# A transformer layer on one core: single-token attention moved beside a head's projection, attention rows merged per head on GpSimd, head turns written out, input sums of the FFN on TensorE

## The chip, the cores and the metric

The kernel runs as one program on one core of a Trainium2 chip. The core has five engines, each with its own instruction stream: TensorE (PE in the profile; its weight loads are PEld), VectorE (DVE), ScalarE (ACT), GpSimd (POOL) and SyncE (SP, which here only issues DMAs). They order themselves by semaphores. The metric is device time in microseconds, lower is better; the kernel before takes 2558.33 us (median of 3 runs, 2557.53 to 2559.42). `L123` is line 123 of the kernel.

## The reference

One decoder layer (D = 1024) is computed for a prompt of 1024 tokens and for 8 samples of one new token each ("sample attention" below), side by side as 1032 columns.

```
h = rms_norm(x); proj = h @ w_in                       # q/k/v of 3 dilated groups, DeltaNet q/k/v/z, gates
o_a = dilated attention, 3 groups, 4 heads of 64: each group gives o, max and denominator;
      merged per head by softmax over the groups' log-sum-exp
      (samples: 8 queries against 129, 129 and 65 keys per group, from caches; one softmax over all groups)
o_b = gated DeltaNet, 8 heads of 128: causal conv(4) + silu, chunked delta rule, gated rms norm
mix = sigmoid(gate_a) * (o_a @ w_branch_a) + sigmoid(gate_b) * (o_b @ w_branch_b)
x = x + rms_norm(mix @ w_out); h = rms_norm(x)
gt, up = split(h @ w_ffn_in); x = x + rms_norm((silu(gt) * up) @ w_ffn_out)
```

Matrix products are done in three passes of split operands (hi and lo parts, `passes`, L271 to L273). Small products and transposes are plain float32, of which one instruction gives two records in the trace.

## The kernel before, in words

The program is a sequence of blocks; a block ends when all engines have reached its end.

1. `norm_block`, then `attention_block`: prompt attention in three groups. Each query tile's unnormalised rows, denominators and maxima go to DRAM (`att_scr`), rows of 4 heads x 66 numbers.
2. `sample_attention_block` (L899 on): a block of its own. TensorE spreads the 8 queries over the partitions by products with selector rows (L1017), VectorE multiplies them with the cached keys (L946) and sums (L950), the softmax follows on 32 rows, and TensorE does 48 products of 2 columns for the outputs (L1048; 96 records). Beside it VectorE merges the prompt's groups (`merge_steps`, L841 to L866), TensorE transposes the merged rows (L828), and they stay in SBUF as `oaT`.
3. `clear_semaphores` (L100): GpSimd clears 75 semaphores one after the other.
4. `heads_block`: the DeltaNet heads. TensorE first transposes the convolution constants (L1746). Head 0's projection follows alone: four tiles (q, k, v, z) of 24 steps, a step being three 344-column products. Then eight turns: turn i computes head i's recurrence, and between its products TensorE does the six tiles (two gates, q, k, v, z) of head i+1's projection as filler. `Filler` and `per_slot` fix by hand how many steps stand between two products of the recurrence; the other engines' streams are laid out by the same step numbers. Turns 0 to 6 are one hardware loop (`Fori`), turn 7 is written out. GpSimd's stream in a turn: load `s_state`, scale it (L2523), later store it.
5. A second clear (100 semaphores), then `pair_block` "mix": its prelude splits `oaT` into hi and lo (ScalarE, then VectorE).
6. `row_block` "wo", then `ffn_block` (a Winograd-like form with 7 products instead of 8). Before its first product it needs sums and differences of blocks of the normed input: `sums_of_x` (L1244 to L1252) and their split (L1263, L1269), one half on VectorE, the other on GpSimd. The splits of the first weight tile follow (L1370 to L1388). Then `row_block` "fo".

What sets the order everywhere is each engine's written stream and the semaphores; there is no scheduler.

Of the kernel before, what the change touches and what calls it, by code (L numbers as in the profile page):

```python
# [21 lines left out]
NS = 8  # L22
# [56 lines left out]
def build(nc, a, o):  # L79

    ctx = ExitStack()
    with ctx:
# [15 lines left out]
        def clear_semaphores():  # L98
# [8 lines left out]
            live.clear()  # L107

# [152 lines left out]
        oaT = sb(oa_stack, "oaT", [P, 2, T])  # L261
# [151 lines left out]
        qT_s = sb(att_stack, "qT_s", [P, NG, 2, NS])  # L413
# [60 lines left out]
        def attention_block():  # L474

            with ExitStack() as s, nc.Block() as block:
# [18 lines left out]
                os_ = sb(s, "a_os", [P, 2, HA, HS]); nm = sb(s, "a_nm", [P, 2, HA])  # L497
# [6 lines left out]
                KVO = (2, 5, 9)  # L504
                done = sums(NT * [KT + 1])
                SPLIT_Q = 4

# [28 lines left out]
                def _(sp):  # L536
# [14 lines left out]
                    for g in range(NG):  # L551
# [5 lines left out]
                        for t in range(NT + 1):  # L557
                            if t == NT:
                                wt(sp, "kv_ev", g, t + 1)
                                dst = o[("kv128_s", "kv512_s", "kv2048_s")[g]][0, :, 0].rearrange("b s h d -> b (s h d)")  # L560
                                sp.dma_start(dst, kv_s[:, g]).then_inc(kvo[g], 16)
                            elif g == 2:
# [10 lines left out]
                        for t in range(NT):  # L573
                            wt(sp, "oe", g, t + 1)
                            wt(sp, "ex", g, t + 1)
                            sp.dma_start(dram_rows(g, t, att_scr[g]),
                                         os_[:, t % 2].rearrange("p h w -> p (h w)")).then_inc(oso[t % 2], 16)
# [97 lines left out]
                def _(act):  # L675
# [12 lines left out]
                    def exps(g, t):  # L688
                        wt(act, "nm", g, t + 1)
                        nk = len(blocks(g, t))  # L690
                        for h in range(HA):
                            x = sc[t % 2][:, h, (2 - nk) * P:]
                            last = nc.scalar.activation(x, x, ACT.Exp, bias=nm[:, t % 2, h:h + 1],
                                                        accum_out=os_[:, t % 2, h, HD:HD + 1])
# [50 lines left out]
                def _(v):  # L745
                    def out_copy(g, t):
                        wt(v, "pv", g, t + 1)
                        for e in range(2):
                            src = banks[4][:].rearrange("p (m e w) -> p m e w", m=2, e=2)[:, :, e, 64 * e:64 * e + 64]
                            last = nc.vector.tensor_copy(os_[:, t % 2, e::2, :HD], src)  # L750
# [23 lines left out]
                    def tile(g, t, fill):  # L774
# [13 lines left out]
                        inc(nc.vector.reduce_max(os_[:, t % 2, :, HD + 1], sc[t % 2][:, :, ks], AX.X), "mx")  # L788
                        wt(v, "mx", g, t + 1)
                        wt(v, "ex", g, max(t - 1, 0))  # L790
                        inc(nc.vector.tensor_scalar(nm[:, t % 2], os_[:, t % 2, :, HD + 1], -1.0, None, ALU.mult), "nm")
# [15 lines left out]

        def merge_steps(s):

            x = sb(s, "m_x", [P, NG, NT, HA, HS]); top = sb(s, "m_top", [P, NT, HA])  # L810
            f = sb(s, "m_f", [P, NG, NT, HA]); z = sb(s, "m_z", [P, NG, NT, HA])
            y = sb(s, "m_y", [P, NT, HA, HD]); y2 = sb(s, "m_y2", [P, NT, HA, HD])
            ld, dv, ac, tr = sem("m_ld"), sem("m_dv"), sem("m_ac"), sem("m_tr")

            def load(sp):
                for g in range(NG):
                    sp.dma_start(x[:, g].rearrange("p t h w -> p t (h w)"),
                                 att_scr[g].rearrange("(t p) w -> p t w", p=P)).then_inc(ld, 16)

            def exps(act):  # L820
                act.wait_ge(dv, 3)
# [1826 lines left out]
```

## Time and profile before

| | us |
|---|---|
| median of 3 runs | 2558.33 |
| the profiled execution | 2558.09 |
| its span (first to last instruction) | 2556.3 |
| TensorE busy | 2265.0 (89%) |
| VectorE busy | 1285.0 (50%) |
| ScalarE busy | 718.7 (28%) |
| GpSimd busy | 66.4 (3%) |
| mean granted clock of TensorE, as a share of full speed | 0.93 |

Engines overlap, so busy times do not add up to the span. "Idle before, releaser" in a row is the time for which the engine waited just before that group and who ended the wait. The granted clock of TensorE has two levels here, 1.0 (2.4 GHz) and 0.5 (1.2 GHz).

### The profile page before, as it was taken

Reading aid. Unit: us, or ns where it says so; the run is one execution under the profiler, and the core shown is the slowest. Engines: PE = TensorE matmul, PEld = TensorE weight load, DVE = VectorE, ACT = ScalarE, POOL = GpSimd, SP = SyncE. Lnnn points to the kernel's source line nnn. Section 1 sums busy time; section 2 is a strip of 40 time slices with the busy share of each in tenths; the row PEclk is TensorE's granted clock in tenths of the full one; section 3 lists DMA queues with packets and bytes.
Section 4 is the critical chain, followed back from the end, with each engine's and each line's share of the span. In section 5 each row is a group of like instructions: output and inputs, shape, how many; then the busy total and the mean of one; then the engine's idle time right before and its main releaser. Section 6 shows DMA issues by size and latency. Waiting matters only on the chain. (4 is left out here: it accounts for less than half of the span.)

```text
span 2556.3 us, 37393 instructions
## 1 busy us (share of the span) xinstructions
PE 2265.0 (89%) x14464; PEld 2099.3 (82%) x14464; DVE 1285.0 (50%) x2344; ACT 718.7 (28%) x1590; POOL 66.4 (3%) x40
## 2 busy tenths in 40 slices
PE   5888988568999999999999779692999999979898
PEld 3677877458999999999999679571999999958676
DVE  4123221244766667666676623358666666531233
ACT  4122221102342323423224210353332233231221
POOL 0000000000000000000000000005000000000000
PEclk9989998558999999999999989896999999989999
DMA  4010201313121212212122144430222222150432
GB/s 147 22 64 11 81 11 51 100 48 77 46 61 43 79 45 59 61 43 79 46 58 69 58 143 138 161 119 25 67 85 81 80 74 74 58 175 23 141 111 63
DMA packets 209582, 190.39 MB, mean 74 GB/s; under 512 B 30243, under 2 KB 180804, under 8 KB 209478
## 3 DMA queue, kind: packets, MB, share of 16 engines
q1 hardware_dynamic: 196090, 144.12, 19.3%
q10 hardware_dynamic: 11120, 36.96, 3.7%
q0 software_dynamic: 2304, 8.39, 1.4%
q8 instruction: 44, 0.72, 0.1%
q14 instruction: 24, 0.20, 0.0%
HBM read 138.05 MB, written 51.59 MB: 74 GB/s over the span
## 5 line engine op out<-in xcount | busy, mean ns | idle before, releaser
L271 PE MATMUL bank<-xT_hi,w_lo 128*128 128x344 f32 x1152 | 393.7, 342 | 3.6 <-DVE w_lo L267 3.6
L273 PE MATMUL bank<-xT_hi,w_hi 128*128 128x344 f32 x1152 | 368.6, 320 | 0.0
L272 PE MATMUL bank<-xT_lo,w_hi 128*128 128x344 f32 x1152 | 368.5, 320 | 0.0
L271 PEld LDWEIGHTS bank<-xT_hi,w_lo 128*128 128x128 f32 x1152 | 218.0, 189 | 3.7 <-issue 3.7
L272 PEld LDWEIGHTS bank<-xT_lo,w_hi 128*128 128x128 f32 x1152 | 218.1, 189 | 0.0
L273 PEld LDWEIGHTS bank<-xT_hi,w_hi 128*128 128x128 f32 x1152 | 217.0, 188 | 0.0
L1293 PE MATMUL bank<-xT_hi,f_hi 128*128 128x258 f32 x704 | 199.5, 283 | 0.0
L1289 PE MATMUL bank<-xT_hi,f_lo 128*128 128x258 f32 x704 | 199.3, 283 | 0.0
L1291 PE MATMUL bank<-xT_lo,f_hi 128*128 128x258 f32 x704 | 199.1, 283 | 0.0
L1289 PE MATMUL bank<-f_thi,f_lo 128*128 128x258 f32 x528 | 149.9, 284 | 47.1 <-DVE f_lo L1388 47.1
L271 PE MATMUL bank<-fo_wh,fo_sl 128*128 128x512 f32 (+1 forms) x396 | 158.0, 399 | 28.4 <-DVE fo_wl L267 23.5
L272 PE MATMUL bank<-fo_wl,fo_sh 128*128 128x512 f32 (+1 forms) x396 | 157.4, 397 | 0.0
L273 PE MATMUL bank<-fo_wh,fo_sh 128*128 128x512 f32 (+1 forms) x396 | 156.9, 396 | 0.0
L1291 PE MATMUL bank<-f_tlo,f_hi 128*128 128x258 f32 x528 | 150.4, 285 | 0.0
L1293 PE MATMUL bank<-f_thi,f_hi 128*128 128x258 f32 x528 | 150.0, 284 | 0.0
L1289 PEld LDWEIGHTS bank<-f_thi,f_lo 128*128 128x128 f32 x528 | 100.5, 190 | 47.2 <-DVE f_lo L1388 47.2
L1289 PEld LDWEIGHTS bank<-xT_hi,f_lo 128*128 128x128 f32 x704 | 133.4, 189 | 0.0
L1291 PEld LDWEIGHTS bank<-xT_lo,f_hi 128*128 128x128 f32 x704 | 133.2, 189 | 0.0
L1293 PEld LDWEIGHTS bank<-xT_hi,f_hi 128*128 128x128 f32 x704 | 132.9, 189 | 0.0
L271 PE MATMUL bank<-a_kv_hi,xT_lo 128*128 128x512 f32 (+1 forms) x216 | 100.4, 465 | 29.6 <-ACT a_kv L705 21.1
L271 PEld LDWEIGHTS bank<-fo_wh,fo_sl 128*128 128x128 f32 (+1 forms) x396 | 71.9, 182 | 50.3 <-issue 24.1
L267 DVE TENSOR_TENSOR fo_sl<-fo_sr,fo_sh 128x1408 fp32r<-128x1408 f32 (+1 forms) x18 | 26.4, 1472 | 149.1 <-ACT fo_sh L1601 149.1
(403 smaller groups left out, 4946.5 us busy)
## 6 DMA issues: line engine op xcount, KB each, us to landing
w_raw<-in_w_in SPq DMA_DIRECT2D x48, 512.0 KB, 3.9
f_raw<-in_w_ffn_in SPq DMA_DIRECT2D x44, 512.0 KB, 4.7
act_scr<-f_y ACTq DMA_DIRECT2D x22, 516.0 KB, 2.7
fo_sr<-act_scr SPq DMA_DIRECT2D x16, 704.0 KB, 6.6
fo_wr<-in_w_ffn_out SPq DMA_DIRECT2D x22, 512.0 KB, 5.5
gate_scr<-gate ACTq DMA_DIRECT2D x16, 516.0 KB, 3.2
a_kv_raw<-in_w_in SPq DMA_DIRECT2D x3, 2048.0 KB, 9.1
mix_ta<-gate_scr SPq DMA_DIRECT2D x8, 516.0 KB, 4.9
```

Of the source, the lines that this page charges most:

```text
L267: return nc.vector.tensor_tensor(dst, src, hi.bitcast(FP), ALU.subtract)
L271: nc.tensor.matmul(out, stat_lo, mov_hi, start=start, stop=False)
L272: nc.tensor.matmul(out, stat_hi, mov_lo, start=False, stop=False)
L273: return nc.tensor.matmul(out, stat_hi, mov_hi, start=False, stop=stop)
L1289: nc.tensor.matmul(bank, lo[j][:, a, k], x_hi[:, k], start=opens and k == 0, stop=False, skip_group_check=True)
L1291: nc.tensor.matmul(bank, hi[j][:, a, k], x_lo[:, k], start=False, stop=False, skip_group_check=True)
L1293: last = nc.tensor.matmul(bank, hi[j][:, a, k], x_hi[:, k], start=False, stop=k == 3, skip_group_check=True)
```

## The change

Four parts.

- **Sample attention and merge.** The block of its own and the first clear are gone; the semaphores of the norm block are cleared by GpSimd during prompt attention. The sample attention's pieces stand in the `prologue` of the heads block, between the steps of head 0's projection. Queries are no longer spread by TensorE: they are written to DRAM and read back broadcast (1 MB for each of two groups, 0.5 MB for the third). Keys and values are loaded apart (1 KB rows), keys into two buffers in turn. The softmax weights of the merge are made by VectorE in the prologue from `att_scr`'s last 8 columns.
- **Merge of rows.** In each head turn GpSimd merges one tile of 128 rows: it loads the rows of groups 1 and 2 into the front of `s_state`, then five operations on 128x256, before it loads `s_state` itself.
- **Head turns** 0 to 6 are written out instead of looped (SP's loads stay a loop). In the mix block's prelude TensorE transposes the merged rows and ScalarE and VectorE split them out of PSUM.
- **FFN input sums.** TensorE adds and subtracts by products with +identity and -identity in PSUM (8 pieces of 16 products of 258 columns), ScalarE and VectorE split out of PSUM; five pieces stand before and three behind the split of the first weight tile.

```diff
-            def pipelined(eng, project, recur, lag=1, between=lambda: None):
-                Filler(project(eng, 0, None)).finish()
-                between()
-                with eng.Fori(0, HB - 1) as i:
+            def pipelined(eng, project, recur, lag, prologue):
+                prologue(Filler(project(eng, 0, None)))
+                for i in range(HB):
                     fill = Filler(project(eng, i + 1, i), done, lag)
                     recur(eng, i, fill)
                     fill.finish()
...
+            SC_STEP, P_STEP, PV_STEP = 112, 126, 132
...
+                    load(0, None, first=True)
+                    constants_load(sp)
+                    sa_load(sp, 0)
+                    merge_load(sp)
+                    load(0, None, first=False)
+                    sa_load(sp, 1)
+                    constants_over(sp)
+                    sa_load(sp, 2)
...
+                @block.tensor
+                    def prologue(fill):
+                        sa_turn_q(pe)
+                        fill.upto(52)
+                        constants_turn(pe)
+                        sa_bias(pe)
+                        fill.upto(SC_STEP)
+                        sa_turn_sc(pe)
+                        fill.upto(P_STEP)
+                        sa_turn_p(pe)
+                        fill.upto(PV_STEP)
+                        sa_products(pe)
+                        fill.finish()
+                        pe.wait_ge(cleared, 1)
...
+                @block.vector
+                    def prologue(fill):
+                        fill.upto(0)
+                        sa_q(v)
+                        fill.upto(1)
+                        constants_take(v)
+                        merge_weights(v)
+                        sa_scores(v, 0)
+                        fill.upto(76)
+                        sa_scores(v, 1)
+                        fill.upto(88)
+                        sa_scores(v, 2)
+                        fill.upto(SC_STEP - 3)
+                        sa_softmax(v)
+                        sa_probs(v)
+                        fill.upto(PV_STEP - 2)
+                        sa_take(v)
+                        fill.finish()
+                        nc.vector.memset(ub[:], 0.0).then_inc(cleared, 1)
...
+                pool.dma_start(x, att_scr[1:, t * P:(t + 1) * P, :DEN].rearrange("g p c -> p g c")).then_inc(x_ld, 16)
+                nc.gpsimd.tensor_tensor(y, y, weight(0), ALU.mult)
+                pool.wait_ge(x_ld, 16 * t + 16)
+                nc.gpsimd.tensor_tensor(of[0], of[0], weight(1), ALU.mult)
+                nc.gpsimd.tensor_tensor(of[1], of[1], weight(2), ALU.mult).then_inc(row, 1)
...
+            BEFORE = 5
...
+                def sums_pe(pe):
+                    pe.wait_ge(signs, 2)
+                    for n in range(8):
+                        if n >= 2:
+                            pe.wait_ge(t_lod, 4 * n - 4)
+                        for m, (bank, terms, opens, _) in enumerate(sums_of_x(n)):
+                            if m == 3:
+                                pe.wait_ge(t_lod, 4 * n + 1)
...
-                    sums_of_x(v, nc.vector, 0)
-                    x_lo(v, nc.vector, 0)
+                    for n in range(BEFORE):
+                        sums_dve(v, n)
                     add(0)
                     for part in range(3):
                         low(0, 0, part)
-                    v.wait_ge(t_lod[1], 4)
+                    for n in range(BEFORE, 8):
+                        sums_dve(v, n)
```

How the streams stand now. TensorE around the sample attention's 2-column products; in the kernel before they are followed by the merged rows' transposes, the two block ends, the constants and then head 0's first product:

```order
L1042 MATMUL bank<-sa_pd,kv_s 128x16 x3
L1048 MATMUL bank<-sa_pT,sa_cache 128x2 x24
L828 MATMUL bank<-ident,m_y 128x128 x16
L899 UNCONDITIONAL_BRANCH
L2529 UNCONDITIONAL_BRANCH
L1746 MATMUL bank<-ident,cs_rows 128x28 x24
L271 MATMUL bank<-xT_hi,w_lo 128x344
```

and in the changed kernel they stand in head 0's last tile, with 12 steps of it behind them:

```order
L277 MATMUL bank<-xT_lo,w_hi 128x344
L278 MATMUL bank<-xT_hi,w_hi 128x344
L1674 MATMUL bank<-sa_pd,sa_own 128x16 x3
L1680 MATMUL bank<-sa_pT,sa_v 128x2 x24
L1674 MATMUL bank<-sa_pd,sa_own 128x16 x3
L1680 MATMUL bank<-sa_pT,sa_v 128x2 x24
L276 MATMUL bank<-xT_hi,w_lo 128x344
```

The 108 plain float32 records (54 instructions) now split the projection instead of preceding it.

VectorE in head 0's projection, before (`w_lo` is the split of a weight tile, `qkv` the convolution of a finished tile):

```order
L1759 TENSOR_SCALAR conv_wt<-bank 128x48
L267 TENSOR_TENSOR w_lo<-w_raw,w_hi 128x1024 x3
L2029 TENSOR_SCALAR qkv<-pre,conv_wt 128x1032
L2034 SCALAR_TENSOR_TENSOR qkv<-conv_state,conv_wt,qkv 128x8
L2037 SCALAR_TENSOR_TENSOR qkv<-pre,conv_wt,qkv 128x1024
```

and in the changed kernel, where the scores of a group (`sa_k`, `sa_sc`) stand before and between them:

```order
L1805 TENSOR_TENSOR m_f<-m_f,m_top 128x32 x3
L1710 TENSOR_TENSOR sa_k<-sa_k,sa_qall 128x2048
L1712 TENSOR_REDUCE sa_sc<-sa_k 128x32
L272 TENSOR_TENSOR w_lo<-w_raw,w_hi 128x1024
L2100 TENSOR_SCALAR qkv<-pre,conv_wt 128x1032
L2105 SCALAR_TENSOR_TENSOR qkv<-conv_state,conv_wt,qkv 128x8
L2108 SCALAR_TENSOR_TENSOR qkv<-pre,conv_wt,qkv 128x1024
L1710 TENSOR_TENSOR sa_k<-sa_k,sa_qall 128x2048
L1712 TENSOR_REDUCE sa_sc<-sa_k 128x32
```

Weight tile 4's split (the `w_lo` here) now stands behind group 0's scores.

VectorE at the start of the FFN, before:

```order
L1244 TENSOR_TENSOR f_x<-xT_hi,xT_lo 128x1032 x4
L1247 TENSOR_TENSOR f_x<-f_x 128x1032
L1248 TENSOR_TENSOR f_x<-f_x 128x1032
L1250 TENSOR_TENSOR f_x<-f_x 128x1032
L1252 TENSOR_TENSOR f_x<-f_x 128x1032
L1269 TENSOR_TENSOR xT_lo<-f_x,xT_hi 128x4x258
L1269 TENSOR_TENSOR f_tlo<-f_x,f_thi 128x4x258 x3
L1370 TENSOR_TENSOR f_sums<-f_raw 128x512
```

and in the changed kernel the last of the first five pieces, the weight tile, and the next piece:

```order
L1068 TENSOR_TENSOR xT_lo<-bank,xT_hi 128x258
L1068 TENSOR_TENSOR f_tlo<-bank,f_thi 128x258
L1167 TENSOR_TENSOR f_sums<-f_raw 128x512
L1169 TENSOR_TENSOR f_raw<-f_raw 128x512
L1170 TENSOR_TENSOR f_sums<-f_sums,f_raw 128x512
L1172 TENSOR_TENSOR f_sums<-f_raw,f_sums 128x512
L1183 TENSOR_TENSOR f_lo<-f_raw,f_hi 128x1024
L1179 TENSOR_TENSOR f_lo<-f_sums,f_hi 128x1536
L1185 SCALAR_TENSOR_TENSOR f_lo<-f_raw,f_hi 128x1024
L1068 TENSOR_TENSOR f_tlo<-bank,f_thi 128x258 x2
```

Twelve operations on 1032 columns with SBUF inputs became 32 on 258 columns with one PSUM input, and the weight tile's seven stand between the fifth piece and the sixth.

## Rows read from the trace of the kernel before

**Rows 1.** Windows, sample attention block: us, then busy us (instructions) of PE, PEld, DVE, ACT, POOL; clock, DMA share, GB/s.

```profile
490.00:571.00 81.00, 56.35 (x193) 46.26 (x193) 39.89 (x75) 2.27 (x4) 0.00 (x0) 0.52 0.37 106
```

**Rows 2.** Windows: the 2-column products, and head turns 2 to 6.

```profile
537.00:562.00 25.00, 25.00 (x105) 24.45 (x104) 13.35 (x17) 0.28 (x1) 0.00 (x0) 0.50 0.00 0
850.00:1380.00 530.00, 529.87 (x3855) 527.57 (x3854) 355.89 (x772) 176.26 (x465) 17.65 (x14) 1.00 0.21 60
```

**Rows 3.** Timeline of PE, 490 to 591: start, us, what [idle before <-releaser].

```profile
490.92 1.44 PE L1010 MATMUL bank<-ident,qT_s 128*8 128x128 f32 x6 [2.79 <-PEq L478]
...
535.10 0.47 PE L1032 MATMUL bank<-ident,sa_S 32*128 32x32 f32 x3 [4.58 <-DVE sa_pselfr L966]
...
537.84 11.75 PE L1048 MATMUL bank<-sa_pT,sa_cache 128*128 128x2 f32 x48
...
583.86 2.76 PE L1746 MATMUL bank<-ident,cs_rows 28*128 28x28 f32 x24 [17.70 <-DMA norm_dv<-in_norm_delta]
590.20 0.63 PE L271 MATMUL bank<-xT_hi,w_lo 128*128 128x344 f32 x1 [3.58 <-DVE w_lo L267]
```

**Rows 4.** Timeline of PE: first transposes of turns 0, 1, 3, 4; warm 2-column products.

```profile
636.95 1.25 PE L2119 MATMUL bank<-ident,qkv 128*128 128x128 f32 x10
729.42 1.73 PE L2219 MATMUL bank<-s_kq,s_state 128*128 128x2 f32 x15
743.79 2.78 PE L2119 MATMUL bank<-ident,qkv 128*128 128x128 f32 x24
957.22 0.49 PE L2119 MATMUL bank<-ident,qkv 128*128 128x128 f32 x3
1063.57 0.60 PE L2119 MATMUL bank<-ident,qkv 128*128 128x128 f32 x4
```

**Rows 5.** Timeline of SP's queue in the sample attention block.

```profile
496.67 17.40 SPq L817 DMA_DIRECT2D m_x<-att_scr  x3
514.12 2.00 SPq L999 DMA_DIRECT2D sa_scr<-sa_self  x1
522.06 2.67 SPq L1002 DMA_DIRECT2D sa_selfr<-sa_scr  x8
```

**Rows 6.** DMA by line (KB each, median us to landing), and instruction loads of turn 0.

```profile
q8 instruction: 6, 0.10, 0.4%
...
w_raw<-in_w_in SPq DMA_DIRECT2D x6, 512.0 KB, 3.9
```

**Rows 7.** Timeline of DVE, 500 to 590.

```profile
525.44 2.28 DVE L950 TENSOR_REDUCE sa_sc<-sa_prod 64x32 f32<-64x2048 f32 x1
539.57 2.29 DVE L862 TENSOR_TENSOR m_y<-m_x,m_f 128x2048 f32<-128x2048 f32 x1
575.46 0.91 DVE L2547 MEMSET ub<- 128x1024 f32 x1 [6.71 <-PEq L100]
588.83 2.36 DVE L267 TENSOR_TENSOR w_lo<-w_raw,w_hi 128x1024 fp32r<-128x1024 f32 x2 [1.12 <-ACT w_hi L264]
606.69 1.28 DVE L2037 SCALAR_TENSOR_TENSOR qkv<-pre,conv_wt,qkv 128x1024 f32<-128x1024 f32 x1
```

**Rows 8.** In the head turns: GpSimd's scaling in turn 3, and all of line 2329 (ns min/median/max).

```profile
960.97 1.89 POOL L2523 TENSOR_TENSOR s_state<-s_state,eg_s 128x1024 f32<-128x1024 f32 x1 [4.70 <-DMA s_state<-in_state_delta]
...
L2329 DVE TENSOR_TENSOR kbe<-k_tok x16: 691/692/2401, 639.5 to 1385.6; 128x512 f32<-128x512 f32 x16
```

**Rows 9.** Timeline at the FFN's start, DVE and PE.

```profile
1748.85 13.09 DVE L1244 TENSOR_TENSOR f_x<-xT_hi,xT_lo 128x1032 f32<-128x1032 f32 x4 [0.61 <-PEq L1444]
...
1802.71 0.42 DVE L1393 TENSOR_TENSOR f_u<-f_u,bank 128x258 f32<-128x258 f32 x1 [8.02 <-ACT f_u L1338]
...
1794.74 0.58 PE L1289 MATMUL bank<-f_thi,f_lo 128*128 128x258 f32 x1 [47.06 <-DVE f_lo L1388]
```

**Rows 10.** Timeline of PE inside the FFN loop.

```profile
1830.00 0.28 PE L1291 MATMUL bank<-f_tlo,f_hi 128*128 128x258 f32 x1
...
1830.60 0.28 PE L1289 MATMUL bank<-f_thi,f_lo 128*128 128x258 f32 x1
```

More of the change, by code:

```diff
@@ L1063, in pair_block @@
-        def pair_block(name, turns, nk_a, rhs_a, rhs_b, w_a, w_b, gates, out_scr, prelude=None):
+        def pair_block(name, turns, nk_a, rhs_a, rhs_b, w_a, w_b, gates, out_scr, prelude=False):
             nk = nk_a + KT
@@ L1119, in _ @@
                     start(pe, 1, *tile_done)
-                    if prelude is not None:
-                        pe.wait_ge(a_lo, 1)
+                    if prelude:
+                        for m in range(2):
+                            for t in range(NT):
+                                last = nc.tensor.transpose(banks[4 + 2 * m + t // 4][:, (t % 4) * P:(t % 4 + 1) * P],
+                                                           merged[:, t, m * P:(m + 1) * P], ident[:])
+                            last.then_inc(a_turned, 1)
+                        pe.wait_ge(a_lo, 3)
                     with pe.Fori(0, turns // 2) as i:
@@ L1155, in _ @@
                     start(act, 16, *stored)
-                    if prelude is not None:
-                        split_weights_hi(act, rhs_a[0][:], prelude).then_inc(a_hi, 1)
+                    if prelude:
+                        split_weights_hi(act, rhs_a[0][:, :, L:], oa_s[:]).then_inc(a_hi, 1)
+                        for m in range(2):
+                            act.wait_ge(a_turned, m + 1)
+                            for b in range(2):
+                                last = split_weights_hi(act, rhs_a[0][:, m, 512 * b:512 * b + 512], banks[4 + 2 * m + b][:])
+                            last.then_inc(a_hi, 1)
                     turns_of(act, act_split, act_join)
@@ L1198, in _ @@
                     v.wait_ge(marked, 1)
-                    if prelude is not None:
+                    if prelude:
                         v.wait_ge(a_hi, 1)
-                        split_lo(v, rhs_a[1][:], prelude, rhs_a[0][:]).then_inc(a_lo, 1)
+                        split_lo(v, rhs_a[1][:, :, L:], oa_s[:], rhs_a[0][:, :, L:]).then_inc(a_lo, 1)
+                        for m in range(2):
+                            v.wait_ge(a_hi, m + 2)
+                            for b in range(2):
+                                c = slice(512 * b, 512 * b + 512)
+                                last = split_lo(v, rhs_a[1][:, m, c], banks[4 + 2 * m + b][:], rhs_a[0][:, m, c])
+                            last.then_inc(a_lo, 1)
                     turns_of(v, dve_split, dve_join)
@@ L1434, in _ @@
                         low(0, 0, part)
-                    v.wait_ge(t_lod[1], 4)
+                    for n in range(BEFORE, 8):
+                        sums_dve(v, n)
                     parity(v, run)
@@ L2470, in _, with load @@
                 def _(sp):
-                    constants_load(sp)
-                    sp.wait_ge(cleared, 1)
-                    def load(h, prev, recur=False):
+                    def load(h, prev, recur=False, first=None):
                         for m, kind in turn_tiles(h).items():
+                            if first is not None and first != (m < 4):
+                                continue
                             if m == 3 and recur:
```

617 lines of the change are left out of this document (324 added, 293 removed).

## The prediction

> **What bounds the kernel now.** I read the page first: TensorE is busy for 89% of the span, VectorE for 50%. The windows by stage then show where TensorE is not the bound. In head turns 2 to 6 it is busy 529.87 of 530 us at full clock [rows 2]: there only its own work counts. The sample attention block is 81 us at a mean clock of 0.52, nearly all at 1.2 GHz [rows 1]. The timeline of TensorE shows a serial stretch from that block's first product at 490.92, over the 2-column products and the constants (17.70 us of waiting, block ends and the clear among it), to head 0's first product at 590.20, which waits 3.58 us for its weights [rows 3]. The FFN's start is the other: TensorE waits 47.06 us for VectorE [rows 9]. The change works on both, and on the full head turns, where it can only do harm or nothing.
>
> **Term A: the sample attention goes beside head 0's projection.** The distance to work on is 490.92 to the first transposes of turn 0 at 636.95 [rows 3, 4], 146 us. I build the new one forward from the block's start at 490.9.
>
> Weights first. They are now SP's first loads: 3.9 us to landing [rows 6], then half of the 2.36 us for one of two tiles on VectorE [rows 7], as much on ScalarE: the first product at about 497.5. The six query transposes (1.44) hide in that.
>
> TensorE's work from there:
> - head 0's projection, unchanged: 636.95 - 590.20 = 46.75 us, cold start included [rows 3, 4];
> - constants 2.76 [rows 3], bias products, the two turns of scores and probabilities: about 7.5 in all with a wait of 2 us for the constants' DMAs;
> - the 2-column products: 2 x 11.75 at 1.2 GHz, with the six key products of the new tokens some 26 us [rows 3]. At full clock 15 records take 1.73 us, 0.115 each [rows 4], so 108 take 12.4. Which of them? In the kernel before TensorE was busy 25.00 of 25 us with them and the clock stayed at 0.50 [rows 2]. They come now after dense products at full clock, so I let it fall after about 5 us: 43 records at 0.115, the rest at 0.245, 21 us, and 2 us for the cold projection products behind. 23, between 12.4 and 29.
>
> Waits. PE's stream stops at step 112 for all three groups' scores. On SP, each spread of queries must wait for VectorE to be done with the last: the second is behind the weight tiles 4 and 5 and the ten small DMAs of the new tokens' scores, of which the first took from 514.12 to 522.06 to be seen landed when large loads stood before it [rows 5]. I get the broadcasts landed at 508, 524 and 533. VectorE needs 2.29 + 2.28 per group [rows 7] plus convolution taps of 1.28 between them: scores ready at 518.5, 529 and 538. TensorE is at step 112 at about 534 and waits 4 us. VectorE then has 8 us of convolution written ahead of the softmax (a silu, a weight split, a scaling, three taps), and TensorE reaches step 126 before the probabilities: the softmax alone kept it waiting 4.58 before [rows 3]. 4.5 us again. The values have landed by then. Sum: 497.5 + 46.75 + 7.5 + 8.5 + 23 = 583, less about 2 us since the small products replace part of the cold start: turn 0 starts at 581. The memset of `ub` (0.91) [rows 7] is done while TensorE does the last 12 steps.
>
> A = 581 - 637 = -56. Bounds: no wait and full clock throughout gives -75; the products all cold and waits of 25 us give -34.
>
> A condition on this is SP's queue: 12 MB pass in about 60 us. It blocked for 17.40 us on three loads when some 8 MB were outstanding [rows 5]. Here at most 3 or 4 MB are, so I give it no term.
>
> **Term B: the head turns.** A turn takes 106.35 us (turn 3, 957.22 to 1063.57), TensorE having no gap at the turn's end in the loop [rows 2, 4]. So removed branches and register work give TensorE nothing. GpSimd's five extra operations of 256 columns take about 1.89/4 each [rows 8], 2.4 us, and come 3 to 7 us into the turn, where VectorE prepares what TensorE transposes next. The scaling of `s_state` moves some 10 us later, and is needed only some 90 us into the turn. Does GpSimd slow VectorE? At the FFN's start VectorE's four additions took 13.09, 3.27 each [rows 9], against 2.29 for twice the columns alone [rows 7]. In turn 3 GpSimd's 1.89 us fell on line 2329, of which one took 2.401 instead of 0.692 [rows 8]. That is turn 3, whose 106.35 us are no longer than turn 0's 106.84 without it [rows 4]. So 2 us of collision at that place cost nothing, and the new collision is of 2 us. B = 0; bounds -2 (0.3 us per turn of faster VectorE chain) and +14 (2 us per turn).
>
> The Trainium skill, "SBUF — State Buffer", section "Who interferes with whom", says that a VectorE instruction with two SBUF inputs and a GpSimd one that reads SBUF lock each other out for a whole instruction. The 3.27 us agree. By it alone each turn would give VectorE up to 2.4 us more, B = +17 if all of it reached TensorE; turn 3 says that it does not.
>
> **Term C: the clears.** The first clear of 75 semaphores is inside A. VectorE waited 6.71 us for it, block ends included, 0.09 per semaphore at most [rows 7]. The second clear has 53 more, those of prompt and sample attention: +4, with nothing beside it. Bounds +3 and +5.
>
> **Term D: the mix prelude.** Sixteen transposes, ScalarE and VectorE in halves, instead of two long splits, while the first mix weights land. 0, within 1.
>
> **Term E: the FFN's start.** Before, 47.06 us of waiting to 1794.74 [rows 9]. Now TensorE does 8 pieces of 16 products. A product of 258 columns comes every (1830.60 - 1830.00)/5 = 0.12 us at full clock [rows 10], 0.24 at half. ScalarE and VectorE each follow with four operations of about 0.42 [rows 9]. A piece is 3.5 us cold and 2.3 warm, as one piece overlaps the next. Start 1750.5 (1.6 us behind the first instruction [rows 9], for the table load and the two identities); pieces 0 to 4 with two cold: 2 x 3.5 + 3 x 2.3 = 14, and 1 for the tail: 1765.5. Then the weight tile without GpSimd beside it: four additions of 512 columns and splits of 1024, 1536 and 1024, at 1.18 per 1024 [rows 7] and a little more for each short one, 7.3 with a wait for ScalarE: 1773. TensorE idles about 7 us in piece 5 and I take it cold again: 3 pieces at 2.3 to 3.5 give 8 and a tail of 1. First product at 1782, and the clock, warmed by the last pieces, saves 2 us behind it. E = 1782 - 1795 - 2 = -15; bounds -20 (all warm) and -8 (all cold, waits of 3 us).
>
> **Sum.** Against the profiled execution's 2558.09 (span 2556.3, the median 2558.33 being 0.24 above): -56 + 0 + 4 + 0 - 15 = -67, 2491 us. Its own range is 2478 to 2507.
>
> **Rivals.**
>
> 1. *The prologue waits for SP.* SP's stream is long and in order; if the broadcasts and the 32-byte rows of the merge statistics land 5 us later each, scores come 15 to 25 us later, VectorE's conv behind them too, and the clock falls in each wait. Price: A = -36 instead of -56, 2511. For it: the 8 us of a 384-byte store behind large loads [rows 5]. Against it: fewer bytes outstanding.
> 2. *GpSimd on VectorE's path.* 2 us per turn over 8 turns, +16: 2507. Against it: turn 3 [rows 8].
> 3. *The loop cost more than it shows.* If the jumps back and the register work cost each turn 1 us (twice what turn 0 has over turn 3), writing seven turns out gives -7: 2484. Against it: no gap at TensorE's turn ends, 529.87 of 530 busy [rows 2]. The Trainium skill, "Runtime: NRT & Kernel Launch", section "Instruction fetch mechanics", says that a taken branch whose target is not in the fetched window stalls for a load and that kernels prefer unrolling for it. This rival is what the rule would do here, and the trace does not show it.
> 4. *Slower: code loads are exposed in the written-out turns.* Turn 0 loads 6 blocks of code on the main instruction queue [rows 6]; now turns 1 to 6 load as many, 36 blocks. If TensorE stood still for each, it would be slower than before from 67/36 = 1.9 us per block on; at 2.1 us it is 2567. Against it: turn 0, with its loads, took 743.79 - 636.95 = 106.84 us, 0.49 more than turn 3 [rows 4], that is under 0.1 us a block.
>
> **How the numbers follow.** Main case 0.62 (2491), rival 1 0.17, rival 2 0.08, rival 3 0.06, rival 4 0.03, and 0.04 for a mix that ends between 2520 and 2560. About 0.2% (5 us) is what a measurement tells from no change. All but rival 4 and half of the last are faster by far more: faster 0.95, same 0.01, slower 0.04. The range takes in rivals 1 to 3 and a main case at its lower bound: 2472 to 2518.
>
> **What would show each step.** A: the first products of head 0 at about 497; waits of TensorE of a few us at step 112 (before the transposes of `sa_sc`) and before those of `sa_S`; the 2-column products in about 20 us with the clock falling in them; turn 0's transposes at 581. If that is past 595, rival 1 it is. B: turns of 106.4 to 106.8 us; past 108 it is rival 2 or 4, which the duration of line 2329's instructions or gaps in TensorE without a releaser tell apart; under 105.5 rival 3. C: GpSimd's clear after the last turn some 4 us longer. E: 33 us from the FFN's first instruction to its first product. The forecast is wrong if A is off by more than 15 us, the only term large enough.

## The result and the profile after

The changed kernel takes 2497.25 us (median of 4 runs, 2493.85 to 2499.89), the kernel before 2557.93 (2556.98 to 2559.42): a ratio of 0.9762, 95% interval 0.9745 to 0.9778. The forecast was 2491, its range 2472 to 2518. The profiled execution took 2498.55 us, its span 2496.8.

Cut at the same instructions of TensorE in both traces, the stretches are:

| stretch (TensorE's first instruction of one to that of the next) | before | after | difference | forecast |
|---|---|---|---|---|
| start to the sample queries' transposes | 490.9 | 488.4 | -2.5 | 0 |
| to turn 0's transposes | 146.0 | 107.7 | -38.4 | -56 (A) |
| the head turns, to the last product | 830.7 | 828.5 | -2.1 | 0 (B) |
| to mix's first product | 20.8 | 25.8 | +5.0 | +4 (C, D) |
| mix, and the projection after it | 258.2 | 256.0 | -2.3 | 0 |
| to the FFN's first product | 48.1 | 31.2 | -16.9 | -13 (E) |
| FFN, to its output projection | 463.4 | 461.7 | -1.7 | -2 (E) |
| output projection, to the end | 298.2 | 297.6 | -0.6 | 0 |

The sum is -59.5, the difference of the spans. One row is short of its forecast by much: the prologue. Its windows in the changed kernel (488 to 596 the whole of it, 563 to 588 the 2-column products, 814 to 1344 five head turns), for [rows 1, 2]:

```profile
core 0: us, PE busy (x) PEld busy (x) DVE busy (x) ACT busy (x) POOL busy (x), PEclk, DMA share, GB/s
488.00:596.00 108.00, 86.79 (x441) 83.02 (x442) 50.43 (x96) 16.04 (x27) 0.46 (x1) 0.72 0.48 125
563.00:588.00 25.00, 25.00 (x113) 24.21 (x113) 2.52 (x5) 0.00 (x0) 0.00 (x0) 0.56 0.08 21
814.00:1344.00 530.00, 530.00 (x3868) 528.52 (x3867) 353.41 (x775) 176.81 (x465) 39.66 (x44) 1.00 0.22 63
```

TensorE's idle time is now 21 us of 108, but the granted clock averages only 0.72 over that window, and 0.56 over the one of the 2-column products. The head turns have no gap. TensorE's timeline, for [rows 3, 4]:

```profile
494.65 0.65 PE L276 MATMUL bank<-xT_hi,w_lo 128*128 128x344 f32 x1 [4.83 <-DVE w_lo L272]
534.38 0.38 PE L1655 MATMUL bank<-ident,sa_sc 128*32 128x128 f32 x2
546.84 0.28 PE L1655 MATMUL bank<-ident,sa_sc 64*32 64x64 f32 x1 [12.07 <-DVE sa_sc L1712]
558.23 0.34 PE L1662 MATMUL bank<-ident,sa_S 32*128 32x32 f32 x3 [1.83 <-DVE sa_S L1736]
564.29 10.34 PE L1680 MATMUL bank<-sa_pT,sa_v 128*128 128x2 f32 x48
575.95 11.75 PE L1680 MATMUL bank<-sa_pT,sa_v 128*128 128x2 f32 x48
596.05 0.71 PE L2190 MATMUL bank<-ident,qkv 128*128 128x128 f32 x5
```

The first product came 6.3 us behind the block's start (forecast 6.6). The wait at step 112, for the third group's scores, is 12.07 us and not 4; the one at step 126 is 1.83 and not 4.5. The 96 records of 2-column products take 22.1 us, 0.215 each in the first 48 and 0.245 in the second. The granted clock was full when they began and fell within 3 us, with TensorE busy without a gap:

```profile
563.00:566.00 3.00, 3.00 (x23) 2.70 (x22) 2.27 (x3) 0.00 (x0) 0.00 (x0) 1.00 0.63 179
567.00:593.00 26.00, 26.00 (x105) 25.53 (x106) 2.16 (x7) 1.41 (x2) 0.00 (x0) 0.50 0.00 0
```

VectorE shows what the scores waited for, and SP's queue why that came late:

```profile
513.78 0.19 DVE L1786 TENSOR_TENSOR m_top<-m_stats 128x32 f32<-128x32 f32 x1 [7.30 <-DMA m_stats<-att_scr]
528.22 2.29 DVE L1710 TENSOR_TENSOR sa_k<-sa_k,sa_qall 128x2048 f32<-128x2048 f32 x1 [3.79 <-DMA sa_qall<-sa_q_scr]
542.18 2.28 DVE L1710 TENSOR_TENSOR sa_k<-sa_k,sa_qall 64x2048 f32<-64x2048 f32 x1 [6.56 <-DMA sa_qall<-sa_q_scr]
```
```profile
504.98 6.59 SPq L1775 DMA_DIRECT2D m_stats<-att_scr  x3
512.24 2.49 SPq L2552 DMA_DIRECT2D w_raw<-in_w_in  x2
514.78 2.30 SPq L1621 DMA_DIRECT2D sa_scr<-sa_self  x1
520.75 2.68 SPq L1624 DMA_DIRECT2D sa_selfr<-sa_scr  x8
523.53 0.35 SPq L1604 DMA_DIRECT2D sa_qall<-sa_q_scr  x1
523.92 1.05 SPq L1629 DMA_DIRECT2D sa_v<-in_cache_kv_w  x2
525.02 3.38 SPq L1631 DMA_DIRECT2D sa_k<-in_cache_kv_w  x1
530.54 0.59 SPq L1604 DMA_DIRECT2D sa_qall<-sa_q_scr  x1
```

Three loads of 32-byte rows kept SP for 6.59 us and VectorE waiting for 7.30. The second spreading of queries was issued at 523.53 and used at 528.22. The third, issued at 530.54 behind 2 MB of values, was used at 542.18.

The second clear and the FFN's start, for [rows 9]:

```profile
1442.49 3.65 PE L901 MATMUL bank<-ident,merged 128*128 128x128 f32 x16 [17.48 <-PEq L100]
1450.38 0.65 PE L276 MATMUL bank<-oa_hi,mix_lo 128*128 128x344 f32 x1 [4.25 <-DVE mix_lo L272]
1710.04 0.58 PE L1054 MATMUL bank<-xT_hi,f_plus 128*128 128x258 f32 x1 [2.70 <-ACT f_minus L1151]
1730.61 0.58 PE L1054 MATMUL bank<-xT_hi,f_minus 128*128 128x258 f32 x1 [6.68 <-DVE f_tlo L1068]
1737.52 0.36 PE L1084 MATMUL bank<-f_thi,f_lo 128*128 128x258 f32 x1 [1.03 <-DVE f_tlo L1068]
```

The 47.06 us of waiting have become pieces of work with one wait of 6.68 in it, forecast at "about 7".

### The profile page after: what moved, and what is told of

It reads as the page before. It is cut to its first block and busy times, and to the rows that moved or that the text cites. A ratio compares the mean times of both kernels' runs of the same rounds, so it can differ in the third digit from the quotient of the medians.

```text
span 2496.8 us, 36400 instructions
## 1 busy us (share of the span) xinstructions
PE 2263.4 (91%) x14544; PEld 2103.3 (84%) x14544; DVE 1238.6 (50%) x2349; ACT 723.6 (29%) x1620; POOL 65.3 (3%) x76
```

## Experiments

All times are medians of 4 runs (6 for the looped kernel), each with its ratio to runs of the kernel before on the same chip. Medians of the kernel before range from 2555.51 to 2557.93 us over these chips, so differences under 3 us between totals say little, and places in the trace decide where effects are small. The block's start itself falls between 486.6 and 490.7 us in the traces of these kernels.

### The order of SP's loads

**Values last.** In the third stage of `load(sp, stage)`:

```diff
                     spread_q(1)
-                    for g in range(2):
-                        sp.dma_start(v_c[:, g], rows(g, 1)).then_inc(v_ld, 16)
                     made(sp, "k_used", 1)
                     sp.dma_start(k_c[0][:64], rows(2, 0)).then_inc(k_ld[0], 16)
                     made(sp, "q_used", 3)
                     spread_q(2)
+                    for g in range(2):
+                        sp.dma_start(v_c[:, g], rows(g, 1)).then_inc(v_ld, 16)
```

> Edit: in SP's stream the third group's keys and the third spreading of queries go ahead of the loads of the first two groups' values (2 MB), which come last. Theory (SP order and bytes ahead of the broadcast cost the wait at step 112): in the changed kernel the third spreading was issued at 530.5 and seen landed at 542.2, the second, with little ahead of it, took 4.7 us. So the third lands at about 535.5, VectorE has the third scores at about 540, TensorE's wait at step 112 falls from 12.3 to about 5.5 us, turn 0 starts about 7 us earlier (589 instead of 596), the total is about 2490; the values, issued at 531 instead of 524, still land before the products want them. Rival (the broadcasts are late because VectorE frees the buffer late and SP's small loads stand before them, bytes don't matter): the third lands at 540 or later, turn 0 moves by 0 to 2 us, total 2495 to 2498.

Measured: 2490.43 us, ratio 0.9735 (0.9719 to 0.9751).

```profile
531.15 0.48 SPq L1604 DMA_DIRECT2D sa_qall<-sa_q_scr  x1
540.79 0.29 PE L1655 MATMUL bank<-ident,sa_sc 64*32 64x64 f32 x1 [6.17 <-DVE sa_sc L1712]
```

The third spreading was issued no earlier (531.15, in the changed kernel 530.54) and TensorE had its scores 6 us sooner. Turn 0 came at 588.73. The bytes ahead of it were the cause; the rival is out.

**Statistics late too.** `merge_load(sp)` moved behind `sa_load(sp, 2)`, the merge weights on VectorE and their exponentials on ScalarE to where TensorE does the 2-column products.

> The values-last kernel, and besides the merge statistics (three DMAs of 32-byte rows, 6.6 us of issue on SP, waited for 7.0 us by VectorE) and the merged rows are loaded as SP's last work of the prologue, and VectorE makes the merge weights while TensorE does the 2-column products. Theory (the small DMAs ahead in SP's queue set when all three spreadings come): first scores at 513.5 instead of 521, second spreading issued at about 515.5 instead of 523.6, third scores ready at about 532, TensorE waits 0 to 1 us at step 112 (6.5 with the values last) and 2 to 4 us before the probabilities' transposes, turn 0 starts at about 579 instead of 588.7, total 2480 to 2482. Rival (the landing times of the small DMAs are long whatever is ahead of them): the third scores come at 537 or later, total 2486 to 2489.

Measured: 2487.62 us, ratio 0.9737 (0.9719 to 0.9756).

```profile
509.34 2.29 DVE L1710 TENSOR_TENSOR sa_k<-sa_k,sa_qall 128x2048 f32<-128x2048 f32 x1 [2.54 <-DMA sa_qall<-sa_q_scr]
523.90 2.29 DVE L1710 TENSOR_TENSOR sa_k<-sa_k,sa_qall 128x2048 f32<-128x2048 f32 x1 [5.25 <-DMA sa_qall<-sa_q_scr]
535.90 0.23 PE L1655 MATMUL bank<-ident,sa_sc 64*32 64x64 f32 x1 [3.00 <-DVE sa_sc L1712]
547.29 0.47 PE L1662 MATMUL bank<-ident,sa_S 32*128 32x32 f32 x3 [2.82 <-DVE sa_S L1736]
```

Against the values-last kernel, the first scores came 7 us earlier, the second group's 5, the third transposes at 535.90 instead of 540.79. Turn 0 came at 584.88, 3.9 us earlier and not 10. The total lies in the rival's range (2486 to 2489), and the third scores between theory (532) and rival (537 or later): the small store of the new tokens' scores still took from 509.40 to 515.73 to be seen landed, and TensorE, which now waits less at step 112, waits 2.82 at step 126, with the clock at half behind it. At 46.8 us behind the block's start, the third scores stand where the forecast had them (538 - 490.9 = 47.1).

### The 2-column products and the clock

**Few of them.** The kernel leaves out the products of seven of the eight tokens:

```diff
-                    for b in range(NS):
-                        for g in range(NG):
+                    for g in range(NG):
```

> Leaves out 90 of the 96 2-column products (one token's stand for all), so the sample attention is not computed for the other tokens. Theory (these products run at half clock and their whole 24 us stands on the path): turn 0 starts 22 to 25 us earlier, at 571 to 574, total 2473 to 2475. Rival (other work ends late too: VectorE's convolution and ScalarE's splits for turn 0 are hidden beside the products): only 10 to 15 us are won, and TensorE waits for VectorE or ScalarE before turn 0.

Measured: 2479.09 us, ratio 0.9695 (0.9679 to 0.9711). Turn 0 came 87.2 us behind the block's start instead of 107.7, and TensorE waited for nobody between the probabilities and it: -20.5. That is nearer the theory (22 to 25) than the rival (10 to 15), but the total, 18.2 us below the changed kernel, misses the theory's 2473 to 2475. Not won were the 36 dense products behind, which took 8.4 us in both kernels, most of it at half clock.

**Dense products between them.** After each token's three products in each half, none or one step (three dense products) of the projection:

```diff
+                        fill.upto(first + (8 * m + b + 1) * 3 // 4)
```

> The same 2-column products, but after each token's six (three per half) one or two steps of head 0's projection, instead of all products first and the last 36 dense ones behind. Theory (the clock is at half because TensorE has only 2-column products for 24 us): with dense products between them the granted clock stays full for most of the stretch, the 108 small ones take 13 to 16 us and the 36 dense ones 6, 20 to 22 us instead of 32.3, turn 0 starts 10 to 12 us earlier, total 2486 to 2488. Rival (the mix does not bring the clock up): stretch unchanged at 31 to 33 us, total 2496 to 2498.

Measured: 2505.77 us, ratio 0.9798 (0.9781 to 0.9814): 8.5 us slower than the changed kernel.

```profile
568.00:598.00 30.00, 30.00 (x118) 29.16 (x118) 0.13 (x1) 0.46 (x1) 0.00 (x0) 0.50 0.00 0
603.51 1.76 PE L2191 MATMUL bank<-ident,qkv 128*128 128x128 f32 x7 [4.52 <-DVE ub L2665]
```

The clock is at half throughout: the rival is right in that the mix did not bring it up, and from the first of these products to the last of the projection it took 34.5 us instead of 32.7. But the total misses the rival's 2496 to 2498 as well. Beyond both expectations VectorE, which takes the products' sums ahead of its last convolution taps, did so only at their end, and TensorE waited 4.52 us for it. In that wait the clock stayed at half, and turn 0 itself took 108.84 us instead of 106.79.

**Wide ones.** The probabilities become the stationary operand, padded with zeros to 32 rows, the values the moving one:

```diff
...
-                                last = nc.tensor.matmul(bank[:, 2 * b:2 * b + 2], v_c[:k, g, b, m * P:(m + 1) * P],
-                                                        pT[:k, g, HA * b + 2 * m:HA * b + 2 * m + 2], start=False,
...
+                        last = nc.tensor.matmul(banks[3][:R, :256], pT[:k, g, R * b:R * b + R], v_c[:k, g, b],
+                                                start=False, stop=(b == NS - 1 and g == NG - 1))
```

> The changed kernel with the sample values' products turned round: 27 products of 256 columns (54 records) and two small transposes stand for 54 products of 2 or 16 columns (108 records). In the kernel before 16 records of this width took 6.97 us at half clock, 0.435 us each, so 0.22 at full. Theory (the clock is at half because TensorE works only on 2-column products): with wide ones it rises within a few us, 54 records take 13 to 16 us instead of 24, the 36 projection products behind 6 instead of 8.3, turn 0 starts 10 to 13 us earlier than 596, total 2484 to 2487. Rival (anything that is not the dense projection keeps the clock at half): 54 x 0.435 = 23.5 us, turn 0 within 2 us of where it was, total 2496 to 2499.

Measured: 2484.87 us, ratio 0.9729 (0.9706 to 0.9753). The first window is this kernel's, the second the changed kernel's:

```profile
564.00:577.00 13.00, 13.00 (x61) 6.41 (x60) 2.50 (x4) 0.00 (x0) 0.00 (x0) 1.00 0.15 41
566.08 10.66 PE L1676 MATMUL bank<-sa_v,sa_pT 128*32 128x256 f32 x48
```
```profile
564.00:587.00 23.00, 23.00 (x104) 22.46 (x103) 1.30 (x2) 0.00 (x0) 0.00 (x0) 0.55 0.05 15
```

TensorE is busy without a gap in both. The granted clock was full ahead of the products in both kernels (from 562.8 in the changed one, from 563.8 with wide ones); it stayed at 2.4 GHz with the wide products and fell to 1.2 within 3 us of 2-column ones. 48 records took 10.66 us, 0.22 each, and turn 0 came at 583.12, 12.9 us earlier. The same busy share stands beside two clocks: PEclk has to be read beside it. The Trainium skill, "TensorE: Matmul & The Clock Gate", section "Part 1: The HAM clock gate (the "warmup" mystery)", says that the clock follows how busy the engine has been; with busy read as the profile's share these two windows contradict it. The two kernels differ in the columns that stream and in the time spent loading weights (PEld busy 6.41 of 13 us against 22.46 of 23). Loading weights all the time does not go with half clock by itself, since PEld is busy for 527.57 of 530 us at full clock in the head turns [rows 2]; beyond that, which property of the 2-column products brings the clock down stays open.

**A filled wait.** 72 products of projection size without use before `sa_turn_sc(pe)`:

> The changed kernel with 72 projection-shaped products without use (344 columns, 0.157 us each at full clock, 11.3 us in all) in the 12.3 us that TensorE waits at step 112. Theory 1 (the wait costs twice: the time, and the half clock behind it): the clock stays full, the 42 dense products behind take 6.6 instead of 9.0 us, the 18 ones 2.8 instead of 4.3. VectorE has the probabilities at 558 as before, so TensorE waits 4 to 5 us there instead of 2.0, and turn 0 starts 1.5 to 4 us earlier: 2493 to 2496. Theory 2 (the clock is not on the path, since VectorE's chain sets the probabilities and the 2-column products start at half clock again): turn 0 moves by less than 1 us, 2496 to 2498.

Measured: 2498.84 us, ratio 0.9778 (0.9761 to 0.9796).

```profile
549.12 0.23 PE L1655 MATMUL bank<-ident,sa_sc 64*32 64x64 f32 x1 [0.66 <-DVE sa_sc L1712]
560.52 0.47 PE L1662 MATMUL bank<-ident,sa_S 32*128 32x32 f32 x3 [4.37 <-DVE sa_S L1736]
```

The clock stayed full through the wait and the 42 products behind took 6.9 us instead of 9.4, but then TensorE waited 4.37 for VectorE, the clock fell in that wait, and turn 0 came 108.1 us behind the block's start (107.7). Theory 2 in its mechanism (the total is 0.8 us above its range): at this place the half clock cost nothing, since VectorE's stream up to the probabilities set the end. It took 11.4 us from the third scores' transposes to those of the probabilities in both.

### The FFN's start

The FFN of before in the changed kernel:

> The changed kernel with the FFN as it was before (sums on VectorE and GpSimd). Term E by itself: the changed kernel reached its first FFN product 16.9 us earlier behind the block before and lost 1.7 us less behind it, so this one is 17 to 19 us slower, 2514 to 2516. Rival (E is what was predicted, -15, and the rest is drift of the stretch from run to run): 2512 or less.

Measured: 2517.90 us, ratio 0.9846 (0.9830 to 0.9863), 20.7 above the changed kernel, which is 1.9 us more than the top of what was expected. In the traces, from the first product of the projection behind mix to the FFN's first, and from there to the output projection, it is 17.7 + 2.0.

And the other way, the new FFN start alone in the kernel before:

> The kernel before with nothing but the new start of the FFN. Theory (term E stands by itself, -17 to -20 as undoing it showed): 2537 to 2541, and prompt attention ends at 490 to 491 us as before. Rival (part of E comes from what the change did ahead of it): less than 15 us gained, 2543 or more. For the prompt attention: if it ends at 487 to 489 here too, its 2.5 us were chance and not the packed rows.

Measured: 2535.95 us, ratio 0.9920 (0.9903 to 0.9937), 21.0 less than the kernel before on that chip and 1 us below the expected range. In the traces it is 15.9 + 1.9. So E is -18 to -20 by the traces and -21 by the medians. The prompt attention, unchanged here, ended at 487.53 (490.92 in the trace of the kernel before), so the 2.5 us of the result come without any change to it: chance from run to run.

### Written-out turns

Turns 0 to 6 in a loop on TensorE, ScalarE and VectorE:

```diff
-                for i in range(HB):
+                with eng.Fori(0, HB - 1) as i:
```

> The changed kernel with head turns 0 to 6 in a loop again on TensorE, ScalarE and VectorE (GpSimd's stay written out). Theory (the loop itself cost what the turns got shorter by): the turns take 106.4 us again instead of 106.14, with all of term B (-2 us) gone: 2499. Rival (the turns are shorter by something else, such as VectorE's prologue or GpSimd's order): they stay at 106.1 to 106.2.

Measured: 2546.84 us, ratio 0.9963 (0.9949 to 0.9978), 49.6 above the changed kernel, which neither side expected. Turns 1 to 6 took 112.9 to 114.9 us, cut at the last product ahead of each. At a turn's start:

```profile
935.48 0.76 PE L2193 MATMUL bank<-ident,qkv 128*128 128x128 f32 x5 [2.98 <-issue]
938.81 0.90 PE L2193 MATMUL bank<-ident,qkv 128*128 128x128 f32 x3 [2.57 <-issue]
```
```profile
937.77 0.58 DVE L2397 TENSOR_TENSOR s_sq<-qkv 128x8 f32<-128x8 f32 x1 [5.45 <-issue]
```

"issue" is a gap without a releaser: the engines had no instructions. The view of DMA queues between 745 and 1340 has them being loaded, which the kernel before did not do there at all:

```profile
q8 instruction: 47, 0.77, 0.5%
q14 instruction: 27, 0.22, 0.1%
```

These are blocks of 16 KB (q8) and 8 KB (q14). In turn 0 (596 to 705), which loads the loop's code for the first time, q8 brings 7 blocks, where the kernel before has 6 in its turn 0 [rows 6]:

```profile
q8 instruction: 7, 0.11, 0.5%
```

From this the next theory.

**TensorE's loop moved by 80 instructions.** 40 products without use in the wait at step 112:

> The looped kernel again, with 40 projection-shaped products without use in TensorE's 12 us wait at step 112 (6.3 us, hidden in it). They are there for their 80 instructions, which move the loop on in TensorE's code. Theory (the loop's place in the code decides): in the kernel before, TensorE's code blocks of 16 KB were loaded 6 times within turn 0, in the looped one 7 times, the first within 1 us of the turn's first instruction, so its loop begins just ahead of a block's end and spans one block more; there every jump back finds its target gone and the loads start again (9 a turn). Moved by 80 instructions the loop begins behind that boundary, the loads in turns 1 to 5 vanish, the turns take 106.4 us instead of 113.8, total 2498 to 2500. Rival (the jump's cost comes from what GpSimd and its DMAs do at the turn's end, which the kernel before did not have): turns stay at 113 to 115 us, total 2545 to 2548.

Measured: 2516.45 us, ratio 0.9836 (0.9820 to 0.9853). The turns took 108.9 us. In the same window:

```profile
q14 instruction: 27, 0.22, 0.1%
```
```profile
928.16 0.17 DVE L2397 TENSOR_TENSOR s_sq<-qkv 128x8 f32<-128x8 f32 x1 [5.39 <-issue]
```

All of q8's loads are gone and 30 of the 50 us with them, by 80 useless instructions. VectorE's 5.39 us are left, so the expected 2498 to 2500 was missed.

**VectorE's too, by 48.**

```diff
+                        for n in range(48):
+                            nc.vector.memset(pad[:, n:n + 1], 0.0)
                         sa_take(v)
```

> The looped, shifted kernel, and VectorE's code moved on as well, by 48 memsets of one column in its 22 us of waiting for the values' products. With TensorE's loop shifted, its code loads within the turns were gone and a turn fell from 113.8 to 108.9 us, but VectorE still stood 5.5 us without a releaser at each turn's start, and the loads of 8 KB blocks went on, 5 a turn; in turn 0 three of them came at 5.2, 38.9 and 96.3 us, against two in the kernel before (28.6 and 89.5). Theory (VectorE's loop, too, spans one block more than it may): it begins some 14 recorded instructions ahead of a block's end, 48 move it behind; the 8 KB loads and the 5.5 us vanish, the turns take 106.4 us, total 2498 to 2500. Rival (what is left is the price of GpSimd's rows and DMAs at the turn's end): turns stay at 108.9, total 2515 to 2518.

Measured: 2495.32 us, ratio 0.9761 (0.9745 to 0.9777), the turns 106.2 us. In the window:

```profile
q14 instruction: 1, 0.01, 0.0%
```

The total is 2.7 us below the range expected, the turns are as expected. That settles it: a loop costs 0.1 us a turn here (106.22 against 106.13 written out) if it stands well in the code, and 7.8 if it stands badly (113.98 on average). GpSimd's rows and DMAs were the same in all three looped kernels, so they are not what made the turns longer. The Trainium skill, "Runtime: NRT & Kernel Launch", section "Instruction fetch mechanics", says that a taken branch whose target is not in the fetched two-page window stalls for a load. The stall of about 3 us agrees. The two pages do not, for TensorE: in the kernel before and in these two its loop was loaded once with 6 block crossings and then ran without a load; with 7 crossings every turn reloaded it.

### All that helped

Values and statistics last, wide products, and the softmax ahead of three convolution taps (`fill.upto(99)` for `fill.upto(SC_STEP - 3)` on VectorE):

> All that helped together: values and merge statistics loaded last, the 27 wide products, and VectorE's softmax ahead of three of its convolution taps. From the late-statistics kernel: third scores turned at 536, 42 dense products 7 to 8 us, the probabilities ready when TensorE gets there (544 instead of 547.3), 18 dense ones 3 to 4, wide products 12.0 as measured, 36 dense and the turning of the sum 6.5: turn 0 at 567 to 571 instead of 584.9, total 2470 to 2474. Rival (VectorE, which now has convolution, merge weights and the sums in a row, becomes the bound): TensorE waits for VectorE or ScalarE after the wide products, turn 0 at 574 or later, total 2477 or more.

Measured: 2467.27 us (2463.31 to 2471.01), ratio 0.9649 (0.9633 to 0.9665), 30 us faster than the changed kernel.

```profile
487.00:564.00 77.00, 68.16 (x389) 58.59 (x389) 51.12 (x94) 16.39 (x27) 0.00 (x0) 0.89 0.67 176
535.11 0.23 PE L1655 MATMUL bank<-ident,sa_sc 64*32 64x64 f32 x1 [2.29 <-DVE sa_sc L1719]
547.31 10.66 PE L1676 MATMUL bank<-sa_v,sa_pT 128*32 128x256 f32 x48
564.36 1.86 PE L2195 MATMUL bank<-ident,qkv 128*128 128x128 f32 x15
```

TensorE waits 2.29 us for the scores and for nothing after, the clock does not fall again after 507 us, and turn 0 comes at 564.36. That is less than the 567 to 571 expected; the dense products behind the scores took 6.9 us and not 7 to 8, and the probabilities were ready 2 us sooner. The rival, VectorE as the bound, did not come.

## Why the prediction was right, and where it was not

**A** was forecast at -56 and is -38.4. From the block's start, turn 0 was to come after 90.1 us and came after 107.7. That is more than the 15 us by which the prediction itself calls A, and with it the forecast, wrong. The time came out inside the range although its largest term failed. The 17.6 us fall on two steps.
- "I get the broadcasts landed at 508, 524 and 533": the third scores were due 47.1 us after the start and came after 58.5, +11.4. The step that failed is "at most 3 or 4 MB are outstanding, so I give it no term". The runs show it: values behind the third spreading gave 6 us back, the statistics moved late 5 more, and then the scores were on the forecast (46.8). The same step gave nothing to the merge statistics, which held SP for 6.59 us and VectorE for 7.30.
- The products and what follows: 31.9 us forecast from the probabilities' transposes on, 37.8 measured. The clock was to fall "after about 5 us" of 2-column products; it fell within 3 us and stayed at half until 593.5, over most of the dense products behind too. The waits ahead were not the reason: with wide products behind the same waits it stayed full, and turn 0 came 23.8 us after the probabilities' transposes instead of 37.8.
- Between them, scores to probabilities, 11.1 forecast (14 steps and 4.5 us of waiting) and 11.4 measured. The split was wrong (1.83 of waiting, the rest products partly at half clock), the sum was not, because VectorE sets it; filling the wait showed that.

This is rival 1: its mark, turn 0 past 595, was met, and its price for A was -36. The total is still 14 us below that rival's 2511 because A was 2.4 us better than its price, the other terms gave more, and the start's 2.5 us came on top.

**B**, forecast 0, is -2.1. Turns of 106.13 to 106.79 us against 106.35 to 106.84, and TensorE was busy for 595 us of 595 (745 to 1340) while 35 blocks of its code were loaded: rivals 2 and 4 are out. The prediction's argument against rival 2 rested on a misreading, though. The operation of 2.401 us is not in turn 3, where both of that line took 0.69 us and ended before GpSimd's scaling began at 960.97. It is in turn 7:

```profile
1385.57 2.40 DVE L2329 TENSOR_TENSOR kbe<-k_tok 128x512 f32<-128x512 f32 x1
1385.53 1.89 POOL L2523 TENSOR_TENSOR s_state<-s_state,eg_s 128x1024 f32<-128x1024 f32 x1 [4.11 <-DMA s_state<-in_state_delta]
```

So turn 3 gave no evidence that a collision costs nothing, and that B came out near 0 is in part luck. Turn 7 gives some: to its last product it took 85.3 us, and 85.1 in the changed kernel, where no operation of that line took over 0.92 us in that turn. The size was off too: GpSimd's five operations took 3.8 us in turn 3 of the changed kernel and not 2.4. But they met little of VectorE's work (the longest operation of that line on 512 columns is 0.99 us where it is else 0.69), and VectorE was busy for 70.6 to 71.1 us in each of turns 0 to 6, no longer than the 70.3 to 72.2 before. The loop's own cost, rival 3, is 0.1 us a turn and not 1. Another 0.15 per turn between the looped kernel before and the looped one with both shifts stays open.

**C and D**, +4 and 0, are +5.0 together. From the last product of the heads to the mix block's first work it took 17.48 us and before 13.0, which makes C +4.4 (the 153 clears themselves took 11.1 us and the 100 before 7.4); the prelude took 7.9 us and before 7.4, so D is +0.5. Mix took 1.9 us less. That this comes from the prelude's transposes is not shown, since with the old prelude and only the FFN changed it took 1.4 us less too.

**E**, -15, is -18.5 in the trace. From the FFN's first instruction (1708.2) to its first product it took 29.3 us and not 33. The first five pieces took 12.0 us and not 14, with one of them at half clock. From the wait of 6.68 on, what was left took 6.9 us and not 9, since all but two of the sixth piece's 16 products stood before the wait and the clock was full again for the last piece (from 1733.6).

The forecast sum is -67 and the spans differ by 59.5: A's +18 and the +1 of C and D are offset by B (-2), E (-3.5), mix and the last stages (-3) and the start's 2.5. The time was near in part because errors of both signs met, which is luck: A alone would have put it at 2509.

## What to carry to other kernels

When small transfers on which an engine waits share a queue with megabytes that nobody needs yet, write the order by who needs what first. Two lines moved in SP's stream were worth 7 us. Read PEclk in every window beside the busy share: a long run of 2-column products kept TensorE busy at half clock here (15 of them in a head turn did not [rows 4]), and turning the operands round, for more arithmetic, halved the time, 12.1 us instead of 24.2. After a loop is moved or the code ahead of it changes, look for "issue" gaps at its turns and for instruction loads in the DMA view; 40 products and 48 memsets without use took 51.5 us off the looped kernel.

## What was not expected of the hardware

- A loop that TensorE ran with no code load for six turns cost 5.0 us a turn more when it crossed 7 instead of 6 of the 16 KB blocks. VectorE's loop did the same with blocks of 8 KB, for 2.7 us a turn, until 48 memsets moved it.
- 48 products of 256 columns took 10.66 us and 96 records of 2 columns 22.1, each with no gap in TensorE; the granted clock over these stretches was 1.00 and 0.55.
- Dense products mixed in threes among the 2-column ones did not raise the clock above 0.50 in 30 us (568 to 598).
- Three loads of 1024 rows of 32 bytes each took SP 6.59 us to issue, two loads of 1 MB 1.05.
